# Experts of a decoder layer: rows gathered directly turned in fp32 for up to four experts, weights in ten buffers

## The reference

```python
logits = t @ w_router + b_router              # t = rms_norm(x, ffn_norm), 512 x 1024
# top group of 4, then the top 2 of its 8 experts, softmax weights e_w times g_top
combine = sum(one_hot(eid, 32) * e_w[..., None], axis=1)
for e in range(32):
    gate, up = split(t @ w_gate_up[e], 2)     # 1024 -> 512 and 512
    y = (silu(gate) * up) @ w_down[e]         # 512 -> 1024
    out = out + combine[:, e:e + 1] * y
return rms_norm(x + out, final_norm)
```

## Time and profile before

| | us |
|---|---|
| median of 3 runs | 1257.01 |
| the profiled execution, in all | 1258.02 |
| its span, first to last instruction | 1256.2 |
| TensorE matmuls busy | 1228.7 (98%) |
| TensorE weight loads busy | 815.3 (65%) |
| VectorE busy | 674.5 (54%) |
| ScalarE busy | 403.5 (32%) |
| GpSimd busy | 424.8 (34%) |

### The profile page before, as it was taken

How to read it: one execution, slowest core, us unless ns; L and a number is a source line. 1 busy time by engine, 2 the same in 40 slices (tenths; PEclk the granted TensorE clock), 3 DMA queues, 4 the chain that set the end, 5 groups by cost and what they waited for, 6 DMA issues and landing times. The chain is left out here.

```text
span 1256.2 us, 19251 instructions
## 1 busy us (share of the span) xinstructions
PE 1228.7 (98%) x7449; PEld 815.3 (65%) x7449; DVE 674.5 (54%) x1140; ACT 403.5 (32%) x983; POOL 424.8 (34%) x455
## 2 busy tenths in 40 slices
PE   8999999999999999999999998999999999999995
PEld 7788989898888989878686783333333333333332
DVE  2744989999998989772534347222222222222225
ACT  2033645546373736522022233111111111111113
POOL 3266765757484754326321116100000000000011
PEclk9999999999999999999999998999999999999999
DMA  9672211122111212323334239999999999999995
GB/s 354 255 291 78 85 68 52 68 85 68 52 68 51 85 50 88 134 97 112 149 124 179 92 114 378 366 423 425 425 425 426 427 425 426 426 426 426 423 420 225
DMA packets 41824, 291.73 MB, mean 232 GB/s; under 512 B 6572, under 2 KB 6700, under 8 KB 23696
## 3 DMA queue, kind: packets, MB, share of 16 engines
q1 hardware_dynamic: 35872, 277.89, 55.1%
q0 software_dynamic: 3552, 8.20, 1.7%
q10 hardware_dynamic: 2320, 4.55, 1.0%
HBM read 272.46 MB, written 22.02 MB: 234 GB/s over the span
## 5 line engine op out<-in xcount | busy, mean ns | idle before, releaser
L2275 DVE TENSOR_SCALAR ee<-ee 128x256 f32<-128x256 f32 x32 | 9.8, 307 | 332.5 <-ACT ee L2156 332.5
L2254 POOL DMA_INDIRECT expert_out<-yy,row_at x30 | 29.4, 980 | 395.5 <-ACT yy L2142 395.5
L706 PE MATMUL bank<-h_sums,ring 128*128 128x256 f32 x384 | 92.2, 383 | 0.0
L706 PEld LDWEIGHTS bank<-h_sums,ring 128*128 128x128 f32 x384 | 71.9, 190 | 9.9
L1943 PE MATMUL bank<-x_rows,select 128*64 128x512 bf16 x464 | 70.1, 382 | 0.0
L706 PE MATMUL bank<-h_sums,weights_0hi 128*128 128x256 f32 x256 | 60.5, 379 | 0.0
L706 PE MATMUL bank<-h_mix,weights_0lo 128*128 128x256 f32 x256 | 58.7, 382 | 1.4 <-PEq L178 1.4
L716 PE MATMUL bank<-weights_0lo,h_mix 128*128 128x128 f32 x512 | 59.2, 277 | 0.0
L716 PEld LDWEIGHTS bank<-weights_0lo,h_mix 128*128 128x128 f32 x512 | 57.9, 192 | 0.3
L2276 DVE RECIPROCAL ee<-ee 128x256 f32<-128x256 f32 x32 | 56.1, 1753 | 1.3 <-DVE ee L2275 0.2
L706 PEld LDWEIGHTS bank<-h_mix,weights_0lo 128*128 128x128 f32 x256 | 47.9, 190 | 10.5 <-issue 4.4
(11 more groups left out here) (416 smaller groups left out, 2823.4 us busy)
## 6 DMA issues: line engine op xcount, KB each, us to landing
weights_0lo<-in_w_gate_up SPq DMA_DIRECT2D x11, 2048.0 KB, 20.6
weights_1down<-in_w_down SPq DMA_DIRECT2D x11, 2048.0 KB, 21.9
weights_0hi<-in_w_gate_up SPq DMA_DIRECT2D x11, 2048.0 KB, 21.5
weights_1hi<-in_w_gate_up SPq DMA_DIRECT2D x11, 2048.0 KB, 22.3
weights_1lo<-in_w_gate_up SPq DMA_DIRECT2D x11, 2048.0 KB, 21.4
weights_0down<-in_w_down SPq DMA_DIRECT2D x11, 2048.0 KB, 20.5
weights_2lo<-in_w_gate_up SPq DMA_DIRECT2D x10, 2048.0 KB, 21.1
ring<-in_w_gate_up SPq DMA_DIRECT2D x10, 2048.0 KB, 22.3
```

The lines of the kernel that those rows point to most:

```text
L706: mm = pe.matmul(bank[:, 0:HALF_T], w[:, k], h[:, k], start=(fresh and k == 0), stop=(k == HALF_K - 1), skip_group_check=True)
L2254: pool.indirect_dma_start(out=half_rows, out_offset=bass.IndirectOffsetOnAxis(ap=row_at[:, e:e + 1], axis=0), in_=yy[e % 2][:], in_offset= ...
```

## The change

Rows are gathered turned: the matmul's stationary operand is a block of 128 channels of `x_rows` and its moving operand `sel`, so that PSUM holds channels by slots. `sel` has the token's root in place of 1, and ScalarE's copy to `xg` multiplies by the channel's ffn gain. Experts are taken in batches: 0 and 1, 2 and 3, then four at a time; a batch's gather is in two halves, after the lo and the hi half of gate/up of the expert before the batch. `x_rows` stays in place, so `x_home`, its store and its reload, `h_rows`, the splitting into pieces and `xr` are gone. The chunks are numbered in the order in which TensorE uses them (lo e, hi e, down e-1) and go round ten buffers, `kv_rows` being the tenth. The loops over experts are written out. The host lays out both weight arrays so that a partition's 16 KB of a chunk are contiguous. The overflow pass follows suit. Cut to its core (`taken` in `gather_half` is the number of copies that must be done before a bank is written again):

```diff
@@ buffers and the order of loads
-WB = 3
+BUFFERS, SETS = 10, 3
+BATCH = 4
+BATCHES = 2 + (NE - BATCH) // BATCH
+        chunks = [weights_0[0], weights_0[1], weights_1[2], weights_1[1], weights_2[0],
+                  kv_rows, weights_0[2], weights_1[0], ring_flat, weights_2[2]]
@@ cross_phase, SyncE
-            load_chunk(sp, g, 0, 0, "gate_up_lo")
+            load_chunk(sp, g, 0, "lo")
             for pair in range(6, 8):
                 weights(pair)
-            load_chunk(sp, g, 1, 1, "down")
+            load_chunk(sp, g, 1, "lo")
             for pair in range(8, 10):
                 weights(pair)
-            load_chunk(sp, g, 0, 0, "gate_up_hi")
+            load_chunk(sp, g, 0, "hi")
             sp.wait_ge(scores, XH)
-            load_chunk(sp, g, 1, 1, "gate_up_hi")
+            load_chunk(sp, g, 1, "hi")
             for pair in range(10, 12):
                 weights(pair)
-            load_chunk(sp, g, 2, 2, "gate_up_lo")
+            load_chunk(sp, g, 0, "down")
+            sp.wait_ge(outs, 2 * XH)
+            load_chunk(sp, g, 2, "lo")
             sp.wait_ge(mm_done, items_of(3 * PAIRS - 1))
-            load_chunk(sp, g, 1, 1, "gate_up_lo")
-            sp.wait_ge(back_got, KC)
-            sp.dma_start(g["x_home"], x_rows[:]).then_inc(g["x_away"], 16)
-            load_chunk(sp, g, 0, 0, "down")
-            load_chunk(sp, g, 2, 2, "gate_up_hi")
-            load_chunk(sp, g, 2, 2, "down")
+            load_chunk(sp, g, 2, "hi")
+            load_chunk(sp, g, 1, "down")
+            load_chunk(sp, g, 3, "lo")
+            load_chunk(sp, g, 3, "hi")
@@ cross_phase, ScalarE and VectorE
-            for t in range(NT):
-                act.activation(h_rows[:, t], h_rows[:, t], ACT.Copy, scale=r_s[:, t:t + 1]).then_inc(scaled, 1)
-            rows_scaled(KC - 2)
-            rows_scaled(KC - 1)
             dve.wait_ge(root_s, 3)
@@ the order of chunks
+def chunk_at(e, part):
+    if part == "down":
+        return 3 * e + 4 if e < NE - 1 else 3 * NE - 1
+    return (3 * e - 1 if e > 1 else 2 * e) + (part == "hi")
...
+def batch_of(e):
+    return e // 2 if e < BATCH else e // BATCH + 1
+def experts_of(b):
+    return range(2 * b, 2 * b + 2) if b < 2 else range(BATCH * (b - 1), BATCH * b)
+def fills_before(b):
+    return 2 * b if b < 2 else 4 * (b - 1)
@@ expert_phase
-        def gather(pe, q, bank, whole=False):
-            parts = [h_rows] if whole else pieces
-            chosen = sel[q] if whole else sel_16[q]
-            for t in range(NT):
-                for i, part in enumerate(parts):
-                    for half in range(2):
-                        mm = pe.matmul(bank[half * SLOTS:(half + 1) * SLOTS, :], chosen[:, t],
-                                       part[:, t, half * 512:(half + 1) * 512], start=(t == 0 and i == 0),
-                                       stop=(t == NT - 1 and i == len(parts) - 1))
+        def gather(pe, bank, ks, columns, width):
+            for n, k in enumerate(ks):
+                for t in range(NT):
+                    mm = pe.matmul(bank[:, n * width:(n + 1) * width], x_rows[:, t, k * P:(k + 1) * P], sel[:, t, columns],
+                                   start=(t == 0), stop=(t == NT - 1))
@@ SyncE
+                for i in range(BUFFERS, 3 * NE):
+                    before, part = chunk_of(i - BUFFERS)
+                    sp.wait_ge({"lo": gu_lo_mm, "hi": gu_mm, "down": dn_mm}[part], before + 1)
+                    load_chunk(sp, g, *chunk_of(i))
-                sp.wait_ge(gathered, EARLY)
-                sp.wait_ge(split, 3 * SPLITS)
-                sp.dma_start(h_rows[:], g["x_home"]).then_inc(x_again, 16)
@@ TensorE
+                def gather_half(b, upper):
+                    es = experts_of(b)
+                    width = SLOTS * len(es)
+                    columns = slice(es[0] % BATCH * SLOTS, es[0] % BATCH * SLOTS + width)
+                    each = 512 // width
+                    ks = range(upper * HALF_K, upper * HALF_K + HALF_K)
+                    if not upper:
+                        pe.wait_ge(picked, b + 1)
+                    for n in range(HALF_K // each):
+                        bank = psum[(upper if each == HALF_K else n)]
+                        taken = KC * b + upper * HALF_K + (n + 1) * each - (KC if each == HALF_K else HALF_K)
+                        after(pe, x_taken, taken)
+                        gather(pe, bank, ks[n * each:(n + 1) * each], columns, width).then_inc(gathered, 1)
...
+                def turn(e):
+                    q, column = e % 2, e % BATCH * SLOTS
+                    then = 1 if e == 0 else batch_of(e) + 1 if e % BATCH == BATCH - 1 and e < NE - 1 else None
+                    pe.wait_ge(x_taken, KC * batch_of(e) + HALF_K)
+                    after(pe, hid, e - 1)
+                    chunk_in(pe, g, e, "lo")
+                    gate_up(pe, column, buffer_of(g, e, "lo"), U[q], range(HALF_K)).then_inc(gu_lo_mm, 1)
+                    if e:
+                        hidden_of(e - 1, 1 - q)
+                    if then:
+                        gather_half(then, 0)
+                    pe.wait_ge(x_taken, KC * batch_of(e) + KC)
+                    chunk_in(pe, g, e, "hi")
+                    gate_up(pe, column, buffer_of(g, e, "hi"), U[q], range(HALF_K, KC)).then_inc(gu_mm, 1)
+                    if then:
+                        gather_half(then, 1)
+                    if e >= NE - 2:
+                        late_table(e - (NE - 2))
+                    if e:
+                        down_of(e - 1, 1 - q)
@@ ScalarE
+                def take_half(b, upper):
...
+                        act.wait_ge(gathered, fills_before(b) + upper * (HALF_K // each) + n + 1)
+                        if b > 1:
+                            act.wait_ge(gu_mm if upper else gu_lo_mm, es[0])
+                        for u in range(each):
+                            k = upper * HALF_K + n * each + u
+                            act.activation(xg[:, k, first:first + width], bank[:, u * width:(u + 1) * width], ACT.Copy,
+                                           scale=g["g_ffn"][:, k:k + 1]).then_inc(x_taken, 1)
@@ VectorE
+                def choose(b):
+                    after(dve, gathered, fills_before(b))
+                    for e in experts_of(b):
+                        column = e % BATCH * SLOTS
+                        for t in range(NT):
+                            mark = dve.tensor_scalar(sel[:, t, column:column + SLOTS], g["slot_row"][:], R["at_slot"][:, t, e:e + 1],
+                                                     R["root"][:, t:t + 1], ALU.is_equal, ALU.mult)
+                    mark.then_inc(picked, 1)
+                def turn(e):
...
+                    if e % BATCH == 0 and e < NE - BATCH:
+                        choose(batch_of(e + BATCH))
                     after(dve, hid_turned, e - 1)
                     dve.wait_ge(ex, e + 1)
@@ finish_phase
-    y1, y2 = g["weights"][2][0], g["weights"][2][1]
+    y1, y2 = buffer_of(g, NE - 3, "lo"), buffer_of(g, NE - 3, "hi")
+    sums = buffer_of(g, NE - 4, "down")
@@ the host's layout
+    laid["w_gate_up"] = np.asarray(inputs["w_gate_up"])[0].reshape(NE, 2, HALF_K, P, -1).transpose(0, 1, 3, 2, 4).reshape(NE, 2, P, -1)
+    laid["w_down"] = np.asarray(inputs["w_down"])[0].reshape(NE, 2, P, 2, -1).transpose(0, 2, 1, 3, 4).reshape(NE, P, -1)
```

More of the change, by code:

```diff
@@ L1772, in _ @@
             for pair in range(out + 1, out + PAIRS):
[L1773 to L1778, removed]
+                products_out(pair, x_t, True)
             for i in range(KC - 2, KC):
@@ L1872, in load_gate_up, with chunk_of @@
-def load_gate_up(eng, g, e, w):
-    load_chunk(eng, g, e, w, "gate_up_lo")
-    load_chunk(eng, g, e, w, "gate_up_hi")
-def load_down(eng, g, e, w):
-    load_chunk(eng, g, e, w, "down")
+def chunk_at(e, part):
+    if part == "down":
+        return 3 * e + 4 if e < NE - 1 else 3 * NE - 1
+    return (3 * e - 1 if e > 1 else 2 * e) + (part == "hi")
+def chunk_of(i):
+    for e in range(NE):
+        for part in ("lo", "hi", "down"):
+            if chunk_at(e, part) == i:
+                return e, part
@@ new lines, in buffer_of, with chunk_in, chunk_source, load_chunk @@
+def buffer_of(g, e, part):
+    return g["chunks"][chunk_at(e, part) % BUFFERS]
+def chunk_in(eng, g, e, part):
+    i = chunk_at(e, part)
+    eng.wait_ge(g["chunk_landed"][i % BUFFERS], 16 * (i // BUFFERS + 1))
+def chunk_source(g, e, part):
+    if part == "down":
+        return g["w_down"][bass.ds(e, 1)].rearrange("o p f -> (o p) f")
+    return g["w_gate_up"][bass.ds(e, 1), 1 if part == "hi" else 0].rearrange("o p f -> (o p) f")
+def load_chunk(eng, g, e, part):
+    at = chunk_at(e, part) % BUFFERS
+    dst = g["chunks"][at][:].rearrange("p c f -> p (c f)")
+    eng.dma_start(dst, chunk_source(g, e, part)).then_inc(g["chunk_landed"][at], 16)
@@ L1976, in down @@
                     at = 1 - n if swapped else n
```

(30 more changed lines are left out.)

311 lines of the change are left out of this document (96 added, 215 removed).

## The result

The changed kernel takes **1259.9 us** (1259.0 to 1261.1), the kernel before, run beside it, 1256.8 (1254.4 to 1257.7): ratio 1.0027, 95% interval 1.0017 to 1.0036. It is slower by 3 us where 14.9 less was predicted. Its profiled execution has a span of 1259.1 us, against 1256.2.

What follows compares the result with a forecast made beforehand. TensorE bounds the kernel before, DMA transfers the changed stage, with gains only at its ends: chunk 95 lands at 1212.8, the late-row tail ends the span at 1241.3, 14.9 under 1256.2; 1257.0 - 14.9 = 1242.1 us, range 1232 to 1252.

Steps and rivals of the forecast that it cites:

- the first term: Expert stage, TensorE: a batch of four experts gathers in 32 matmuls, 6.8 us, 1.7 per expert.
- its own formula: TensorE time per expert: 14.28 less 3.39 for the old gather and transposes, plus 1.7 for the new gather, 12.6 us.
- Transfers: Expert stage, DMA queue: 15.27 us per expert before, 5.055 us per 2 MB chunk after; it sets the stage's pace.
- 0.035 was taken: Weight transfers: the contiguous w_down layout saves 0.1 us per down chunk, 0.035 per chunk.
- the prediction's sum: Weight transfers: chunk 13 lands at 798.3, 82 chunks follow at 5.055 us, chunk 95 lands at 1212.8.
- Front: Start of the stage: first gather 6.3 us, first gate/up 768.4, idle 3.3, chunk 13 lands at 798.3.
- Tail: After the last chunk: stored-row branch ends at 1239.0, late-row branch at 1241.3; the later counts.
- the branch that ends: Tail: chunk 95 at 1213.8, down 31, 16 late matmuls, squares and last products, ending at 1241.3.
- A: Rival, expert stage: DMA queue not at its limit, TensorE's 12.6 us sets the pace, 1207 us; chance 2%.
- B: Rival, expert stage: clock falls in TensorE's gaps, TensorE becomes the bound, slower, near 1275 at s = 0.45; chance 4%.
- C: Rival, front: stalls at experts 0 to 4 leave the queue idle 9 to 14 us, 1251 to 1256; chance 7%.
- the chance of 0.93 for faster: Whole kernel: chance that the change is faster; same was given 0.02, slower 0.05.

Runs made afterwards that it cites:

- Runs 2: Changed kernel with the gathers of experts 4 to 31 over two of four row tiles (tokens 256 to 511 left out): 1253.5 us, ratio 0.9968.
- run 10: Changed kernel with the gather in bf16, only the upper 16 bits of x and of the selection (rows rounded): one execution, 1239.96 us.
- run 5: Changed kernel with every gather over two of four row tiles (tokens 256 to 511 left out of all experts): 1245.9 us, ratio 0.9906.
- run 11: Changed kernel with bf16 upper-half gather, second choice behind expert 0's SwiGLU, late and own rows together per tile, clock-keeping matmuls: 1235.38 us, ratio 0.9832.

## Why the prediction was wrong

**The step that failed** is the first term: "32 matmuls of 128x256 ... Eight weight loads of that form take 1.70, 0.2125 each, so 32 take 6.8 us, 1.7 per expert". The time of an instruction was right (14.0 / 64 = 0.219). The count was not: the code has 32 matmuls, the engine gets 64 instructions, and a batch's gather costs 14.0 us. It could be read from the rows. In the earlier trace rows half a gate/up is x16, and `gate_up` writes eight fp32 matmuls for it (four k-blocks, two output halves), while the bf16 `gather` is x24 for the 24 that its loops write (four tiles, three pieces, two halves). In the earlier trace rows the fp32 gather of one expert is x16 for eight. The very row that the duration came from is x8, for a loop over `HALF_K` = 4 matmuls. The text ahead of the prediction makes the same slip: its "16 matmuls" of `gate_up`, `down` and the late rows are instructions, its "24 bf16 matmuls" are both. So a duration per instruction of the trace was multiplied by a count of matmuls in the source. With 14.0, its own formula gives 14.28 - 3.39 + 3.50 = 14.4 us per expert (measured 14.43), above the 14.28 of before and below the 15.27 of the transfers: no gain in the stage, no waits for weights, and an end that only the front and the tail can move. Runs 2 and 5 take that one factor away, and run 10 takes it away together with half of each instruction's time. Each time TensorE starts to wait for weights, and the time falls to 1253.5, 1245.9 and 1240.0, against the forecast of 1242.1.

**Transfers: right.** 15.27 us per expert before; after 5.07 per chunk, 15.2. What the new layout of `w_down` gives no run isolates: over chunks 40 to 88 the pace goes from 5.087 before to 5.072 after, 0.015 where 0.035 was taken, but with the same layout it is 5.046 and 5.041 in runs 10 and 11. From chunk 13 to 95, the stretch of the prediction's sum, these two take 5.08 and 5.06 per chunk, where 5.055 was predicted.
In the full stretches the transfers move 425 to 427 GB/s, in every run. The Trainium skill's cap for the SBUF side is 435 (DMA: Bandwidth & Descriptors, "Where 436 GB/s comes from"); the trace agrees with it as a cap that is nearly reached, and its own pace was the one to take.

**Front: the structure right, the sizes not.** Opening 760.07 (predicted 760.05), `choose(0)` 1.88 (1.9), TensorE's wait 3.0 (3.3). First gather 9.58 against 6.3, the next ones 3.77 against 2.0: the same factor of two, in full where the clock is at full and less in the first gather, whose further instructions run at full clock already. Not foreseen at all was that the 3 us wait takes the clock away once more: half speed from 793.9 to 797.3, 1.7 us. Hi of expert 1 ended at 798.8, not 790.3, chunk 13 landed at 807.0, not 798.3.

**Tail: right in kind.** The second gather of each pair comes back in 5.3 to 6.7 us (9.5 taken; 11.75 before), but not only for want of a reload: here the gathers go out at 1228.0, when the last chunk has landed at 1227.8. In run 10, where the gathers go out from 1203.4 on and weights land until 1210.8, it takes 9.6 to 9.7: 9.5 was close for a kernel bound by its transfers. Down 31 with the late rows is the branch that ends. From the start of down 31 to the end it took 27.3 us; the prediction had 27.5 from the last landing. But its start is set by TensorE, at 1231.75, and not by a landing at 1213.8.

**Rivals.** A (12.6 us per expert sets the pace) never could be; run 5 shows the transfers bind first. B, the low clock in a stage that waits, was given 4%. Runs 5, 10 and 11 speak against it: waits of up to 1.5 us before a gate/up and up to 1.8 before a down product, with the granted clock at 1.00 in all those stretches. Only at the two ends of the stage, in longer waits, did it cost something. The Trainium skill's case (TensorE: Matmul & The Clock Gate, "HAM oscillation — how this bites in real kernels") lost its clock in waits longer than its bursts, which isn't this pattern. The longer waits here mostly did lose it: 3.06 us before expert 0's hidden rows, 2.45 and 2.13 us before down 31 in runs 5 and 11, but not 2.33 us there in run 10. What decides between these no run shows. C (the front eats the gain) had the right place and part of the price: 7.0 us at the front. The outcome that came, TensorE remaining the bound because the gather is no cheaper, was not among the rivals, and the chance of 0.93 for faster had no room for an error in the largest term.

## What to carry to other kernels

Before a duration from a trace is multiplied by a count from the source, calibrate the count: find a line of the same type in the trace, and divide its xcount by the matmuls that the code writes there. Here that factor is 2 for fp32 matmuls and 1 for bf16 ones and for fp32 transposes, and it decided between two bounds 7% apart. And a producer of later work (a `choose` for experts 4 to 7) belongs behind the operation that the next matmul waits for: its 3.65 us cost 4.5 to 4.9, more than its length, because the clock went with the wait.

## What the runs showed of the hardware

An fp32 matmul of 128x256 costs nearly four times that of bf16: two instructions of 0.219 us against one of 0.117. A wait of TensorE of 2.13 us (run 11), 2.45 us (run 5) or 3.06 us (the change) was followed by 3.4 us at half clock, which made 16 instructions of 128x512 take 5.3 us instead of 3.6; one of 2.33 us (run 10) was not, and waits of 1.3 to 1.8 us in the busy stage never cost it. With the queue full, weight transfers kept nearly one pace, 5.04 to 5.09 us for 2 MB over chunks 40 to 88, whether they landed 15 us after issue (the change) or 47 (run 11).
